# Six of eight chunks of a mixing stage turned by VectorE and device memory in place of TensorE

## What is computed

```python
h = rms_norm_2(x, mix_norm[l])
proj = h @ w_in[l] + b_in[l]
q, k, v, f_logit, xr, gr, g_attn, g_rnn = jnp.split(proj, SPLIT_POINTS, axis=-1)
q = rms_norm_2(q.reshape(B, S, N_HEADS, HEAD_DIM_2), q_norm[l])
k = rms_norm_2(k.reshape(B, S, N_HEADS, HEAD_DIM_2), k_norm[l])
log_f = jax.nn.log_sigmoid(f_logit.astype(jnp.float32))
y_attn = forgetting_attention(q, k, v, log_f) @ w_o_attn[l]
xr = causal_depthwise_conv(xr, conv_w[l], conv_b[l])
yr = rg_lru(xr, lru_w_a[l], lru_b_a[l], lru_w_x[l], lru_b_x[l], lru_lambda[l]) * jax.nn.gelu(gr)
y_rnn = yr @ w_o_rnn[l]
merged = jax.nn.sigmoid(g_attn) * y_attn + jax.nn.sigmoid(g_rnn) * y_rnn
x = x + merged @ w_out[l]
```

## Time and profile before

| | |
|---|---|
| median of 3 runs | 1863.47 us (1863.38 to 1864.08) |
| the profiled execution's own time | 1863.22 us |
| its span in the trace | 1861.4 us |
| TensorE busy | 1850.0 us, 99% |
| VectorE busy | 1238.5 us, 67% |
| ScalarE busy | 1061.4 us, 57% |
| first and second mixing stage in the trace | about 801 to 1063 us and 1421 to 1684 us |

### The profile page before, as it was taken

How to read it: one execution, slowest core, us unless ns; L and a number is a source line. 1 busy time by engine, 2 the same in 40 slices (tenths; PEclk the granted TensorE clock), 3 DMA queues, 4 the chain that set the end, 5 groups by cost and what they waited for, 6 DMA issues and landing times. The chain is left out here.

```text
span 1861.4 us, 24532 instructions
## 1 busy us (share of the span) xinstructions
PE 1850.0 (99%) x9552; PEld 1565.7 (84%) x9552; DVE 1238.5 (67%) x1807; ACT 1061.4 (57%) x1536; POOL 95.6 (5%) x163
## 2 busy tenths in 40 slices
PE   8999999999999999999999999999999999999999
PEld 7889998879999888888888888888888888888887
DVE  6868777677777755557876654665555788665555
ACT  6756555666555643468855544363535886546352
POOL 2000000000000001000010010101010001000100
PEclk9999999999999999999999999999999999999999
DMA  8445564537556567644555466676675446456664
GB/s 265 156 140 200 172 207 165 174 114 230 184 182 204 184 201 251 210 172 159 179 195 204 161 223 227 218 260 215 212 234 196 159 158 230 152 190 209 219 234 136
DMA packets 164493, 361.89 MB, mean 194 GB/s; under 512 B 7782, under 2 KB 20683, under 8 KB 163867
## 3 DMA queue, kind: packets, MB, share of 16 engines
q1 hardware_dynamic: 154400, 327.24, 51.8%
q0 software_dynamic: 9520, 32.89, 6.0%
q10 hardware_dynamic: 459, 0.20, 0.0%
HBM read 348.73 MB, written 11.58 MB: 194 GB/s over the span
## 5 line engine op out<-in xcount | busy, mean ns | idle before, releaser
L1335 ACT ACTIVATE w_hi<-raw 128x1024 fp32r<-128x1024 f32 x620 | 633.3, 1054 | 451.1 <-PE bank L515 192.6
L2089 DVE TENSOR_TENSOR w_lo<-raw,w_hi 128x1024 fp32r<-128x1024 f32 x620 | 733.9, 1223 | 196.1 <-ACT w_hi L1335 189.2
L513 PE MATMUL bank<-w_hi,r_hi 128*128 128x512 f32 x1344 | 531.3, 395 | 1.2 <-DVE r_lo L2113 0.6
L515 PE MATMUL bank<-w_hi,r_lo 128*128 128x512 f32 x1344 | 523.9, 390 | 0.0
L514 PE MATMUL bank<-w_lo,r_hi 128*128 128x512 f32 x1344 | 523.2, 389 | 0.0
L513 PEld LDWEIGHTS bank<-w_hi,r_hi 128*128 128x128 f32 x1344 | 252.4, 188 | 56.4 <-DVE r_lo L2113 2.4
L515 PEld LDWEIGHTS bank<-w_hi,r_lo 128*128 128x128 f32 x1344 | 252.3, 188 | 53.5
L514 PEld LDWEIGHTS bank<-w_lo,r_hi 128*128 128x128 f32 x1344 | 252.6, 188 | 50.0
L513 PE MATMUL bank<-w_hi,z_hi 128*128 128x512 f32 x656 | 258.9, 395 | 1.5 <-DVE z_lo L2089 0.7
L515 PE MATMUL bank<-w_hi,z_lo 128*128 128x512 f32 x656 | 255.7, 390 | 0.0
L514 PE MATMUL bank<-w_lo,z_hi 128*128 128x512 f32 x656 | 255.6, 390 | 0.0
(11 more groups left out here) (231 smaller groups left out, 1557.4 us busy)
## 6 DMA issues: line engine op xcount, KB each, us to landing
raw<-in_w_in SPq DMA_DIRECT2D x79, 1024.0 KB, 5.1
raw<-in_ffn_w_down SPq DMA_DIRECT2D x44, 1024.0 KB, 7.9
raw<-in_w_up SPq DMA_DIRECT2D x40, 1024.0 KB, 5.2
raw<-in_ffn_w_gate SPq DMA_DIRECT2D x40, 1024.0 KB, 5.6
raw<-in_ffn_w_up SPq DMA_DIRECT2D x40, 1024.0 KB, 8.1
raw<-in_w_down SPq DMA_DIRECT2D x22, 1024.0 KB, 4.8
raw<-in_w_out SPq DMA_DIRECT2D x16, 1024.0 KB, 5.1
by_block<-qk POOLq DMA_DIRECT2D x20, 512.0 KB, 3.3
```

The source lines that it names most:

```text
L513: pe.matmul(out_, lh, rh, start=start, stop=False, skip_group_check=True)
L515: return pe.matmul(out_, ll, rh, start=False, stop=stop, skip_group_check=True)
L1335: A_(w_hi[:, n % NH, :], raw[:, u % NS, HALF * h:HALF * (h + 1)], ACT.Copy).then_inc(hi_ready, 1)
L2089: return V.tensor_tensor(dst, src, hi.bitcast(F32), ALU.subtract)
```

## The change

For chunks 0 to 5 TensorE no longer transposes. VectorE transposes 32x32 blocks out of the staging area (`turn_chunk(n, t)`, twice a chunk), GpSimd's queue carries them out and back (`chunks_moved`), and `store` reads them from `qk` or `v` in place of a bank. Chunks 6 and 7 stay with `turned`. There is one area for blocks and one for moved chunks (chunk 5 has its own pair in `v`), and reads of chunk `n` are issued after both stores of chunk `n - 1`. The staging area of a chunk is free once its blocks are transposed. The three lists of the mixing stage are new from top to bottom.

```diff
+        chunk_blocks = [qk_flat[:, 0:1024]] * 5 + [v_flat[:, 0:1024]]
+        chunk_moved = [qk_flat[:, 1024:2048]] * 5 + [v_flat[:, 1024:2048]]
...
+            def chunks_moved(l):
+
+                for n in range(6):
+                    pool.wait_ge(prod_turned, 2 * chunk_at(l, n) + 2)
+                    pool.dma_start(by_block[n % 2], chunk_blocks[n]).then_inc(prod_out, 16)
+                    pool.wait_ge(prod_out, 16 * (chunk_at(l, n) + 1))
+                    if 0 < n < 5:
+                        pool.wait_ge(qk_ready, 8 * LAYERS + 16 * l + 2 * n)
+                    if n == 5:
+                        pool.wait_ge(lru_conv, 4 * l + 4)
+                    for a in range(4):
+                        pool.dma_start(chunk_moved[n][32 * a:32 * a + 32, :].rearrange("c (b r) -> c b r", b=4),
+                                       by_block[n % 2].rearrange("(b c) (a r) -> a c b r", b=4, a=4)[a]
+                                       ).then_inc(prod_in, 16)
...
                 blocks_moved(2 + 2 * l)
+                chunks_moved(l)
                 pool.wait_ge(f_copied, l + 1)
...
                 part(3, 0)
+                lru_linear(0)
                 part(3, 1)
                 part(3, 2)
-                turned(1)
                 part(3, 3)
-                lru_linear(1)
-                turned(2)
                 part(4, 0)
                 part(4, 1)
                 part(4, 2)
                 part(4, 3)
+                lru_linear(1)
                 part(5, 0)
-                turned(3)
...
                 def store(n, b):
-                    act.wait_ge(turned_q, q0 + 2 * n + b + 1)
+                    if n < 6:
+                        if n == 5 and b == 0:
+                            act.wait_ge(qk_ready, q0 + 10)
+                        act.wait_ge(prod_in, 64 * (chunk_at(l, n) + 1))
+                        back = chunk_moved[n].rearrange("p (b m q) -> p m b q", b=4, q=32)
...
+                def turn_chunk(n, t):
+
+                    if n < 4:
+                        dve.wait_ge(rnn_staged, 8 * l + 2 * n + t + 1)
+                    else:
+                        dve.wait_ge(qn_ready, 8 * LAYERS + 4 * l + n - 3)
+                    if 0 < n < 5:
+                        dve.wait_ge(prod_out, 16 * chunk_at(l, n))
+                    V.transpose(chunk_blocks[n].rearrange("p (a m t q) -> p t a m q", a=4, t=TB, q=32)[:, t, :, :, :],
+                                staged(n)[:, t, :].rearrange("p (m a q) -> p a m q", a=4, q=32)).then_inc(prod_turned, 1)
...
                 def copy_v(c, t):
+                    if c == 0 and t == 0:
+                        dve.wait_ge(prod_out, 16 * (chunk_at(l, 5) + 1))
+                    if c == 0 and t == 1:
+                        dve.wait_ge(qk_ready, q0 + 12)
```

More of the change, by code:

```diff
@@ L1206, in _ @@
                 part(0, 2)
+                part(0, 3)
                 forget_logits()
-                part(0, 3)
                 part(1, 0)
+                part(1, 1)
                 forget_turn()
-                turned(0)
-                part(1, 1)
                 part(1, 2)
                 part(1, 3)
-                lru_linear(0)
                 part(2, 0)
@@ L1867, in store @@
                         col = C2_QN if n < 6 else C2_KN
+                        if n < 6:
+                            A_(qk[:, tile:tile + 2, :].rearrange("p k (t b q) -> p (k t) b q", t=TB, q=32),
+                               back[:, 4 * b:4 * b + 4, :, :], ACT.Identity, scale=par2[:, l, col:col + 1]
+                               ).then_inc(qk_ready, 1)
+                            return
                         A_(qk[:, tile:tile + 2, :], two(E + b), ACT.Identity, scale=par2[:, l, col:col + 1]
@@ L1873, in store @@
                         cb = C2_BREST + (KT if n % 2 else 0) + tile
-                        last = A_((gr_t if n % 2 else xr_t)[:, tile, :], bank[E + b][:, i * SEQ:(i + 1) * SEQ],
+                        last = A_((gr_t if n % 2 else xr_t)[:, tile, :].rearrange("p (t b q) -> p t b q", t=TB, q=32),
+                                  back[:, 4 * b + 2 * i:4 * b + 2 * i + 2, :, :],
                                   ACT.Gelu_apprx_tanh if n % 2 else ACT.Identity, bias=par2[:, l, cb:cb + 1])
@@ L1947, in _ @@
                 stage_chunk(1, 1)
+                stage_chunk(2, 0)
+                store(0, 0)
+                store(0, 1)
                 hi(u + 8, 0)
-                lru_root(0)
-                stage_chunk(2, 0)
+                stage_chunk(2, 1)
                 hi(u + 8, 1)
                 hi(u + 9, 0)
-                store(0, 1)
+                lru_gates_(0)
+                hi(u + 9, 1)
+                hi(u + 10, 0)
                 store(1, 0)
-                stage_chunk(2, 1)
+                lru_root(0)
@@ L1980, in _ @@
-                lru_gates_(2)
-                squares_of(5)
-                hi(u + 15, 0)
-                lru_root(2)
-                hi(u + 15, 1)
-                squares_of(6)
-                hi(u + 16, 0)
-                deviations(5)
-                hi(u + 16, 1)
-                store(4, 0)
-                store(4, 1)
-                hi(u + 17, 0)
-                hi(u + 17, 1)
+                hi(u + 15, 0)
+                squares_of(5)
+                lru_gates_(2)
+                hi(u + 15, 1)
@@ L1993, in _ @@
+                hi(u + 16, 0)
+                hi(u + 16, 1)
+                lru_root(2)
+                hi(u + 17, 0)
+                deviations(5)
+                hi(u + 17, 1)
+                store(3, 0)
+                store(3, 1)
                 hi(u + 18, 0)
                 lru_high(2)
+                hi(u + 18, 1)
+                squares_of(6)
                 lru_gates_(3)
-                hi(u + 18, 1)
                 hi(u + 19, 0)
-                squares_of(7)
                 hi(u + 19, 1)
@@ L2965, in _ @@
-                stage_chunk(4, 0)
-                lru_taps(2)
-                stage_chunk(4, 1)
-                lo(u + 11, 0)
-                lo(u + 11, 1)
-                lo(u + 12, 0)
-                lo(u + 12, 1)
+                lo(u + 11, 0)
+                turn_chunk(3, 0)
+                lo(u + 11, 1)
+                stage_chunk(4, 0)
+                lo(u + 12, 0)
+                turn_chunk(3, 1)
+                stage_chunk(4, 1)
+                lru_taps(2)
+                lo(u + 12, 1)
@@ L2992, in _ @@
                 lru_scan(2)
-                lru_low(2)
                 lo(u + 17, 0)
                 lo(u + 17, 1)
+                scale(5)
+                lru_low(2)
                 lo(u + 18, 0)
+                turn_chunk(5, 0)
+                turn_chunk(5, 1)
+                stage_chunk(7, 0)
                 sums(6)
-                stage_chunk(7, 0)
                 lo(u + 18, 1)
                 stage_chunk(7, 1)
-                copy_v(0, 0)
+                lru_gains(3)
                 lo(u + 19, 0)
@@ L3004, in _ @@
                 scale(6)
-                lru_gains(3)
+                lo(u + 20, 0)
+                copy_v(0, 0)
                 sums(7)
-                lo(u + 20, 0)
-                scale(7)
                 lo(u + 20, 1)
@@ L3011, in _ @@
                 copy_v(1, 0)
-                copy_v(1, 1)
                 lo(u + 21, 0)
```

292 lines of the change are left out of this document (149 added, 143 removed).

## The result

The changed kernel takes 1868.11 us (median of 20 runs, 1864.06 to 1872.55), the kernel before, run beside it on the same chip, 1864.11 us (20 runs, 1863.38 to 1865.42). The ratio is 1.0021, with a 95% interval of 1.0014 to 1.0028: slower, by 4.0 us, where 13 were forecast. The runs also scatter over 8.5 us where they had scattered over 2. The profiled execution is one of the better ones: its run took 1866.88 us, 1.9 more than its span.

What follows compares the result with a forecast made beforehand. TensorE's issued work was taken as the bound. Per layer, 7.4 us later at part(6, 2), less 1.8 for blocks, plus 1.4 late wait gives 7.0; two layers add 14 to 1863.22, forecast 1877 us, range 1866 to 1890.

Steps and rivals of the forecast that it cites:

- step 5: First mixing layer: chunk 2 may be read only at 863.2 and is there 0.3 + 9.5 us later, at 873.0.
- Steps 1 and 2: First mixing layer: chunk 0, transposed by 824.9, is back at 838.3; TensorE waits 1.5 us before lru_linear(0).
- Step 3: First mixing layer: chunk 1's last transposition ends at 844.0, it is back at 857.4; ScalarE reaches store(1, 0) at 853.
- Step 4: First mixing layer: store(1, 1) is done at 863.2, stage_chunk(3, 0) stands behind it, and part(5, 0) waits 1.4 us.
- step 6: First mixing layer: store(2, 0) and lru_gates_(1) end at 880.3, so TensorE waits 3 us before lru_linear(2).
- Step 7: First mixing layer: VectorE's list through lo(u + 13, 1) is done at 892.4, so part(6, 2) waits 4.8 us.
- Rival (c): Mixing stage: GpSimd's queue order and a TensorE clock lowered by waits make it over 1885 us, say 1892; chance 0.13.
- The late wait: After chunk 5's trip, copy_v(0, 1) is done 1.4 us after gate_part(0, 0)'s second tile wants it (0 to 2.5 us).
- The blocks: Twelve `turned` blocks taken from TensorE, six a layer, at 0.90 us each: 10.8 us less.
- rival (a): Mixing stage: trips under 8 us in place of 13.4, so no waits and the whole gain, 1852.4 to 1854 us; chance 0.07.
- case (d): The forecast itself: waits of 7 to 14 us a layer against 5.4 us removed, 1867 to 1885 us; chance 0.70.
- (b): Mixing stage: trips of 11 to 12 us, waits about equal to the 5.4 us of blocks a layer, 1859 to 1867 us; chance 0.10.

Runs made afterwards that it cites:

- ScalarE's first edit: Against the changed kernel, stage_chunk(3, 0), stage_chunk(3, 1), lru_root(0) and hi(u + 10, 1) moved ahead of store(1, 0) on ScalarE: 1857.90 us, ratio 0.9970.

## Why the prediction came out as it did

The forecast was slower, with the waits of TensorE in the mixing stages as its reason. Both are so. The time was 9 us too long: 13 us of loss were forecast and 4.0 measured, and the step that failed is step 5, the price of a set of reads.

- **Steps 1 and 2, chunk 0.** A trip of 13.4 us was forecast; the write took 5.1 (826.06 to 831.17), the reads 4.7, and 10.3 it was in all from the last transposition. Chunk 0 was back at 836.1, and the 1.5 us before `lru_linear(0)` did not come.
- **Step 3, chunk 1.** Back at 857.4 forecast, at 856.4 in the trace: here the weight loads ran beside it, and its write took 6.3 us (843.64 to 849.97), more than the 3.3 of the earlier trace rows, the reads 6.1. A price too low and one too high met, so the hit is luck.
- **Step 4.** `store(1, 1)` at 863.2 forecast, 862.4 measured; wait of `part(5, 0)` 1.4 forecast, 1.2 and 1.4 measured.
- **Step 5 is the one that failed:** "it is there 0.3 + 9.5 us later". It was there 0.55 + 4.5 us later. That is the mis-sized term: 9.5 us for a set of reads, which measured 4.5 us where it counted most and 4.5 to 8.5 over all twelve sets, and with it step 6 (a wait of 3 us before `lru_linear(2)`, none measured) falls away. The run with reads twice and the one with more load bring the wait back with the price.
- **Step 7.** `part(6, 2)`: 4.8 us forecast, 3.5 measured. Part of the shortfall of steps 5 and 6 was made up by what I had priced at nothing, the clock: 1.6 us a layer. Rival (c) had named the mechanism. The waits of the walk add up to 10.7 us where the prediction has 11.0; the sum doesn't hang on it, since its 7.4 us are 892.4 less 884.97.
- **The late wait:** 1.4 us (0 to 2.5) a layer forecast; in the profiled execution none, and 0.9 a little later, at `turned(7)`; up to 4.3 in executions of other kernels. The place was right, the range too narrow.
- **The blocks:** 0.90 us each forecast, and borne out by the run without them to within 0.7 us in twelve.
- **ScalarE's waits at L1898:** 2, 4 and 5 us forecast for chunks 0, 1 and 2; none, 3.3 and 0.6 measured. The 9 to 10 us from a first read's issue to the store were 4.5 to 6.2.

**Why the price was wrong.** The earlier trace rows were measured where weight loads run beside the reads: the DMA engines moved 0.68 of the time on the mean there, and their share was 1.04 from 672.9 to 682, during one such set. I gave that stretch's price to one at 0.48, though the prediction names the difference under rival (a). At the moment that counts it was 0.50, and no weight load was in flight when chunk 2's reads were issued: none was issued between 854.0 and 865.8, and the one before had landed at 861.4. The busy share alone is not the price, though. Chunk 1's reads, at 0.99, took 4.6 us each, where the sets of the feed-forward parts, at 0.95 to 1.06, took 4.6 to 9.2; there a weight load was issued 1.0 to 2.3 us into every set, behind another in flight, and for chunk 1 only 3.8 us into it. That the load is the cause is shown by the run with the extra transfer and, for the last read of a set, by the one with the load held back.

Is it ScalarE's standing before `store(1, 0)` that clears the DMA engines, since `hi` and with it the loads stop? The kernel with ScalarE's first edit answers that. It doesn't stand there, and its reads of chunk 2 were as quick, 2.8 to 2.9 us each, with a load in flight until 861.0:

```profile
855.30 1.28 ACT L1898 ACT_TABLE_LOAD   x1
856.59 1.71 ACT L1898 ACTIVATE qk<-qk,par 128x256 f32<-128x256 f32 x4
...
DMA to landing us min/median/max: 2.8/2.9/2.9
...
858.86:863.31 4.45, 4.45 (x22) 3.73 (x21) 3.50 (x4) 2.93 (x4) 2.18 (x4) 1.00 0.53 141
```

So the quick reads don't need that wait. The kernel before, too, issues no weight load for 12 us near this place (846.6 to 858.6). What sets the times of the loads was not tried.

**The rule for one transfer.** A read of 128 KB took 2.9 us at a busy share of 0.50, up to 6.4 at 0.90, and 4.7 to 9.2 in the feed-forward part. By the Trainium skill (DMA: Bandwidth & Descriptors, Anatomy of one DMA) it is 2.3, an estimate by its formula for one DMA. A set is then complete after 3.95 us, as the prediction has it; all twelve sets took longer (4.5 to 8.5 us) and all took less than 9.5, and for chunk 2 the estimate was the nearer of the two. The Trainium skill (DMA: Bandwidth & Descriptors, Queues, rings and completion order, under Arbitration) also says that a DMA engine takes turns between the queues that it has work for, a packet at a time; the run with the load held back is in line with it, with 3.7 us against 5.1 for the slowest read, but no run here shows the turns themselves.

**The rivals.** (a), the whole gain, is what the run without latency gives (1854.5), so its price for a kernel without waits was right; its premise, trips under 8 us, was not (10.3 us for chunk 0 and 13.0 for chunk 1). The measured time lies at the lower edge of the forecast's own case (d), 1867 to 1885. Its mechanism is rather that of (b), trips shorter but not short enough, which got 0.10 and 1859 to 1867 us; the slow steps of TensorE, which (b) had left out, are 3 us of the 1868.1.

## What to carry to other kernels

A transfer's duration belongs to the stretch in which it was measured: before it goes into a sum, put the busy share of the DMA engines in both stretches beside it, and ask which loads will be in flight when it is issued and which will be issued into it. A wait put on an in-order engine is paid by what stands behind it in its list: here four calls moved ahead of the waiting one turned a change that cost 4 us into one that gains 6. With four more moved (three on ScalarE, one on VectorE) it gained 9, which the intervals do not tell from 6. And when a wait of the bounding engine is removed by filling or reordering alone, look for where it comes out again before counting it.

## What the runs showed of the hardware

- TensorE's clock fell to its lower level, 1.2 GHz, when it had stood idle: behind all 13 waits of 3.3 to 8.3 us (start to start, in the profiled executions of all these kernels) came 7 to 14 steps of about 0.43 us; behind the eight of 2.0 to 3.0 us it did so three times. A wait of 3.5 us cost about 5 (the balance above). The Trainium skill (TensorE: Matmul & The Clock Gate, Wait — 56ns, not 53.3ns?) has 426.7 ns for a step of 512 columns at that level; the trace agrees (two steps from 887.79 to 888.64, 0.85 us).
- Of four reads of 128 KB issued 0.55 us apart (chunk 5, 22 sets), the last took 6.5 to 8.2 us where a 1 MB weight load was issued ahead of it, 3.3 to 6.0 where it was issued behind it, and 3.0 and 3.7 where it was held back; the first took 3.0 to 4.2 in all of them.
- At a busy share of the DMA engines of 0.99 such reads took 4.6 us each (chunk 1, first layer), at 1.04 in the feed-forward part 5.9 to 7.5 (the set of the earlier trace rows): the share alone does not give the landing.
- 1 MB more on the DMA engines in each mixing stage, used by nobody and issued beside chunk 2's reads, made the kernel 8.8 us longer in its profiled execution (one run).
